# The opening of a two-layer decoder step: unit 0 and x in turns on one queue, squares on ScalarE, two more banks, five products of a cleared tile

## The reference

```python
def layer(i, h, ...):
    mix, buf_new, S_new = mixer(rmsnorm(h, norm1[i]), buf, S, pos0, w_in[i], ...)   # w_in: 1024 x 2560
    h = h + mix
    hn = rmsnorm(h, norm2[i])
    f = swiglu(hn, ...) if i % 2 == 0 else moe(hn, ...)    # 8 experts, top 2
    h = h + f
    gate = sigmoid(h @ w_ple_gate[i]); e = p_l @ w_ple[i]
    h = h + gate * e

def rmsnorm(x, g):
    y = xf * lax.rsqrt(jnp.mean(xf * xf, axis=-1, keepdims=True) + NORM_EPS)
    return y * g
```

## Time and profile before

| | us |
|---|---|
| median of 3 runs | 898.3 (895.4 to 898.36) |
| profiled execution | 897.86 |
| its span | 894.9 |
| TensorE busy in the span | 871.5 (97%) |
| VectorE, ScalarE, GpSimd busy | 692.8, 540.8, 172.9 |

### The profile page before, as it was taken

The page is one execution under the profiler, slowest core; times in us unless marked ns, Lnnn a source line. Parts: engine busy times, 40 slices in busy tenths (PEclk is TensorE's granted clock), DMA queues, the critical chain, the costliest instruction groups (busy, mean ns, idle before and its releaser), DMA issues.

```text
span 894.9 us, 14463 instructions
## 1 busy us (share of the span) xinstructions
PE 871.5 (97%) x5919; PEld 758.6 (85%) x5919; DVE 692.8 (77%) x793; ACT 540.8 (60%) x659; POOL 172.9 (19%) x190
## 2 busy tenths in 40 slices
PE   6999999999999999999999999999999999999995
PEld 5999999999999999999887777777777777777794
DVE  5796676555555588786869888899898989898976
ACT  5446555343435455346557878787777777876752
POOL 5456321100110013664411010002000110010012
PEclk9999999999999999998999999999999999999998
DMA  9993565545553644944439999999999999999801
GB/s 338 371 326 94 176 218 203 192 153 199 190 179 131 219 163 175 301 139 151 163 107 355 412 337 362 407 363 397 359 390 364 393 389 366 402 358 392 335 2 48
DMA packets 50739, 237.59 MB, mean 265 GB/s; under 512 B 4866, under 2 KB 8226, under 8 KB 42944
## 3 DMA queue, kind: packets, MB, share of 16 engines
q1 hardware_dynamic: 44672, 215.51, 64.5%
q0 software_dynamic: 5280, 20.04, 7.8%
q10 hardware_dynamic: 720, 1.10, 0.4%
HBM read 226.38 MB, written 9.63 MB: 264 GB/s over the span
## 4 chain that ended last, share of the span: by engine, by line
PE 79%; DVE 9%; DMA 4%; ACT 4%; issue 2%; POOL 1%; SPq 0%; ACTq 0%; DVEq 0%; POOLq 0%
PE bank L726 12%; PE bank L727 12%; PE bank L728 12%; PE bank L1091 8%; PE bank L1092 8%; PE bank L1093 8%; PE bank L1117 4%; PE bank L1116 4%; PE bank L1118 4%; DVE wlo L1575 4%; ACT whi L1282 2%; DMA raw<-in_moe_w_up 1%; DMA xg<-tokens,from_row 1%; PE bank L852 1%; PE bank L1049 1%
## 5 line engine op out<-in xcount | busy, mean ns | idle before, releaser
L1575 DVE TENSOR_TENSOR wlo<-raw,whi 128x1408 fp32r<-128x1408 f32 (+2 forms) x292 | 468.7, 1639 | 95.7 <-ACT whi L1282 95.6
L1282 ACT ACTIVATE whi<-raw 128x1408 fp32r<-128x1408 f32 (+2 forms) x292 | 392.5, 1377 | 146.0 <-PE bank L728 83.3
L726 PE MATMUL bank<-xh,whi 128*128 128x264 f32 x672 | 194.1, 289 | 9.3 <-DVE xl L1586 8.6
L727 PE MATMUL bank<-xl,whi 128*128 128x264 f32 x672 | 191.7, 285 | 0.0
L728 PE MATMUL bank<-xh,wlo 128*128 128x264 f32 x672 | 191.4, 285 | 0.0
L1091 PE MATMUL bank<-whi,xeh 128*96 128x512 f32 (+1 forms) x384 | 143.7, 374 | 0.7 <-DVE hid L1880 0.6
L1092 PE MATMUL bank<-wlo,xeh 128*96 128x512 f32 (+1 forms) x384 | 143.5, 374 | 0.0
L1093 PE MATMUL bank<-whi,xel 128*96 128x512 f32 (+1 forms) x384 | 143.2, 373 | 0.0
L726 PEld LDWEIGHTS bank<-xh,whi 128*128 128x128 f32 x672 | 127.8, 190 | 11.0 <-DVE wlo L1967 8.5
L727 PEld LDWEIGHTS bank<-xl,whi 128*128 128x128 f32 x672 | 127.9, 190 | 0.2
L728 PEld LDWEIGHTS bank<-xh,wlo 128*128 128x128 f32 x672 | 127.2, 189 | 0.0
(11 more groups left out here) (264 smaller groups left out, 1198.6 us busy)
## 6 DMA issues: line engine op xcount, KB each, us to landing
raw<-in_moe_w_gate SPq DMA_DIRECT2D x32, 1408.0 KB, 8.9
raw<-in_moe_w_up SPq DMA_DIRECT2D x32, 1408.0 KB, 9.4
raw<-in_moe_w_down SPq DMA_DIRECT2D x40, 1024.0 KB, 8.2
raw<-in_w_in SPq DMA_DIRECT2D x17, 1024.0 KB, 6.4
raw<-in_ffn_w_down SPq DMA_DIRECT2D x16, 704.0 KB, 4.3
raw<-in_ffn_w_gate SPq DMA_DIRECT2D x10, 1024.0 KB, 4.9
raw<-in_ffn_w_up SPq DMA_DIRECT2D x10, 1024.0 KB, 4.9
raw<-in_w_o SPq DMA_DIRECT2D x8, 1024.0 KB, 10.6
```

The source lines that it names most:

```text
L726: pe.matmul(out, w_hi, x_hi, start=start, stop=False)
L727: pe.matmul(out, w_hi, x_lo, start=False, stop=False)
L1282: act.activation(unit_hi(u), unit_raw(u), ACT.Copy).then_inc(hi_ready, 1)
L1575: dve.tensor_tensor(unit_lo(u), unit_raw(u), unit_hi(u).bitcast(F32), ALU.subtract).then_inc(lo_ready, 1)
```

## The change

- Unit 0 is loaded in four quarters (two rows of chunks each), and after each quarter two chunks of x, all on SyncE's queue; the first constants are issued behind unit 1. ScalarE's queue issues only the gains. Each quarter has its own semaphore; ScalarE and VectorE work quarter, two chunks of x, quarter and so on.
- All eight squares are made on ScalarE: two ahead of unit 1's halves, six behind them. GpSimd only adds.
- Chunks 4 and 5 (unit 2) use banks 5 and 6 instead of 0 and 1 and don't wait for an evacuation; the wait begins with chunk 6.
- TensorE first issues five fp32 products of the cleared tile `sq` into bank 7.

```diff
+FIRST_PARTS = (4, 2)
+        def unit_part(x, u, part, at=LOW_AT):
+            n = COLS[u] // FIRST_PARTS[u]
+            return x[:, at[u] + part * n:at[u] + (part + 1) * n]
+        def main_bank(n):
+            return n + 1 if n in (4, 5) else n % 4
...
-            first_rows(0, top_in)
-            first_rows(1, raw_landed[0])
-            sp.dma_start(const[:, 0:FIRST_CONST], t["const"][:, 0:FIRST_CONST]).then_inc(first_in, 16)
+            for i in range(4):
+                first_rows(i, top_in[i] if i < 3 else raw_landed[0])
+                sp.dma_start(h[:, 2 * i:2 * i + 2, :], t["x"][:, 2 * i:2 * i + 2, :]).then_inc(x_in[i], 16)
             for u in range(1, 3):
                 load_rows(u, t["w_in_rows"][:, 256 * u:256 * (u + 1)])
+                if u == 1:
+                    sp.dma_start(const[:, 0:FIRST_CONST], t["const"][:, 0:FIRST_CONST]).then_inc(first_in, 16)
...
-                if at >= 4:
+                if at >= 6:
                     pe.wait_ge(acc_free, n - 3)
-                out = bank[at % 4][:, 0:T]
+                out = bank[main_bank(at)][:, 0:T]
...
+            pe.wait_ge(still, 1)
+            for _ in range(5):
+                pe.matmul(bank[7][:, 0:T], sq[:, 0, 0:P], sq[:, 0, :], start=True, stop=True)
...
             act.dma_start(gains[:, :, :], t["gains"]).then_inc(gains_in, 16)
-            for i in range(4):
-                act.dma_start(h[:, 2 * i:2 * i + 2, :], t["x"][:, 2 * i:2 * i + 2, :]).then_inc(x_in[i], 16)
             act.wait_ge(still, 1)
             act.activation(rstd[0:1, 0:1], sq[0:1, 0, 0:1], ACT.Sqrt)
-            hi_half(0, 0)
-            for m in range(DC):
-                h_final(act, 0, m)
-                part(0, m)
-                if m == 1:
-                    hi_half(0, 1)
-            for half in range(2):
-                hi_half(1, half)
-            for m in range(5, DC):
-                act.activation(first[:, m, :], h[:, m, :], ACT.Square).then_inc(first_sq, 1)
+            for i in range(4):
+                hi_part(0, i)
+                for m in (2 * i, 2 * i + 1):
+                    h_final(act, 0, m)
+                    part(0, m)
+            for m in range(2):
+                first_square(m)
+            for i in range(2):
+                hi_part(1, i)
+            for m in range(2, DC):
+                first_square(m)
...
-            lo_half(0, 0)
-            for m in range(DC):
-                finish(0, m)
-                if m == 1:
-                    lo_half(0, 1)
-            for half in range(2):
-                lo_half(1, half)
+            for i in range(4):
+                lo_part(0, i)
+                for m in (2 * i, 2 * i + 1):
+                    finish(0, m)
+            for i in range(2):
+                lo_part(1, i)
...
             pool.memset(sq[:, 0, :], 0.0).then_inc(still, 1)
-            for m in range(5):
-                pool.wait_ge(x_in[m // 2], 16)
-                pool.tensor_tensor(first[:, m, :], h[:, m, :], h[:, m, :], ALU.mult).then_inc(pool_step, 1)
-                steps += 1
-            pool.wait_ge(pool_step, steps)
             for m in range(0, DC, 2):
-                if m >= 4:
-                    pool.wait_ge(first_sq, m // 2 * 2 - 3)
+                pool.wait_ge(first_sq, m + 2)
                 pool.tensor_tensor(first[:, m, :], first[:, m, :], first[:, m + 1, :], ALU.add).then_inc(first_sums, 1)
```

More of the change, by code:

```diff
@@ L652, in dense, with first_rows @@
                     load(first + j, t[name][layer][:, n * c0:n * (c0 + w)], n * w)
-            def first_rows(half, landed):
+            def first_rows(part, landed):
                 _, _, n, _, w = W_IN[0]
-                n //= 2
-                dst = unit_half(raw, 0, half).rearrange("p (k w) -> p k w", k=n)
-                src = t["w_in_rows"][half * n * P:(half + 1) * n * P, 0:w]
+                n //= FIRST_PARTS[0]
+                dst = unit_part(raw, 0, part).rearrange("p (k w) -> p k w", k=n)
+                src = t["w_in_rows"][part * n * P:(part + 1) * n * P, 0:w]
                 sp.dma_start(dst, src.rearrange("(k p) w -> p k w", p=P)).then_inc(landed, 16)
@@ L763, in first_pair @@
                 L = unit_lo(u).rearrange("p (k w) -> p k w", k=DC)
-                for half in range(2):
-                    pe.wait_ge(lo_ready if half else first_lo, u + 1)
-                    for k in range(4 * half, 4 * half + 4):
+                parts = FIRST_PARTS[u]
+                rows = DC // parts
+                for part in range(parts):
+                    if part == parts - 1:
+                        pe.wait_ge(lo_ready, u + 1)
+                    else:
+                        pe.wait_ge(first_lo, u * (FIRST_PARTS[0] - 1) + part + 1)
+                    for k in range(rows * part, rows * (part + 1)):
                         if u == 0:
@@ L774, in first_pair @@
                                 mm.then_inc(unit_used if m else acc_full, 1)
-                    if u and half == 0:
+                    if u and part == 0:
                         side_step(0, "norm1")
@@ L1436, in experts, with hi_part, first_square @@
                     part(5, m)
[L1438 to L1442 removed]
+            def hi_part(u, part):
+                last = part == FIRST_PARTS[u] - 1
+                act.wait_ge(raw_landed[LANDING[u]] if u or last else top_in[part], 16)
+                act.activation(unit_part(whi, u, part, HIGH_AT), unit_part(raw, u, part),
+                               ACT.Copy).then_inc(hi_ready if last else first_hi, 1)
+            def first_square(m):
+                act.activation(first[:, m, :], h[:, m, :], ACT.Square).then_inc(first_sq, 1)
             act.dma_start(gains[:, :, :], t["gains"]).then_inc(gains_in, 16)
[L1445 to L1446 removed]
             act.wait_ge(still, 1)
             act.activation(rstd[0:1, 0:1], sq[0:1, 0, 0:1], ACT.Sqrt)
[L1449 to L1458 removed]
+            for i in range(4):
[9 more added lines that the diff above has]
+                first_square(m)
             for l in range(DEPTH):
@@ L1962, in over_expert, with lo_part @@
                     dve.tensor_tensor(h[:, m, :], h[:, m, :], osg[:, :], ALU.add).then_inc(o_done, 1)
-            def lo_half(u, half):
-                dve.wait_ge(hi_ready if half else first_hi, u + 1)
-                dve.tensor_tensor(unit_half(wlo, u, half), unit_half(raw, u, half), unit_half(whi, u, half, HIGH_AT).bitcast(F32),
-                                  ALU.subtract).then_inc(lo_ready if half else first_lo, 1)
-            lo_half(0, 0)
-            for m in range(DC):
-                finish(0, m)
-                if m == 1:
-                    lo_half(0, 1)
-            for half in range(2):
-                lo_half(1, half)
+            def lo_part(u, part):
+                last = part == FIRST_PARTS[u] - 1
+                if last:
+                    dve.wait_ge(hi_ready, u + 1)
+                else:
+                    dve.wait_ge(first_hi, u * (FIRST_PARTS[0] - 1) + part + 1)
+                dve.tensor_tensor(unit_part(wlo, u, part), unit_part(raw, u, part), unit_part(whi, u, part, HIGH_AT).bitcast(F32),
+                                  ALU.subtract).then_inc(lo_ready if last else first_lo, 1)
+            for i in range(4):
[4 more added lines that the diff above has]
+                lo_part(1, i)
             for l in range(DEPTH):
```

13 lines of the change are left out of this document (3 added, 10 removed).

## The result

The changed kernel takes **899.15 us** (median of 14 runs, 896.8 to 903.5); the kernel before takes 896.84 (median of 14; one of them, 1073.8 us, is left out of every mean here). The ratio is 1.0029, with a 95% interval of 1.0016 to 1.0042: slower, by 1.4 to 3.8 us, a small loss but clear of the noise. The forecast was 897.1 against the profiled 897.9, a small gain. The profiled execution of after took 901.1 us, its span 899.4.

The account below looks back on a forecast made before the run. TensorE, busy 871.5 of 894.9 us, was taken as the bound. Unit 2 starting earlier gave -2.2 us, a clock fall +1.4, so -0.8 against the profiled 897.9: forecast 897.1, range 893.6 to 899.8.

Parts of the forecast that it names:

- nothing else in this diff touches the rest: Whole kernel behind the opening: nearly every microsecond TensorE gains in its opening comes off the end, nothing else changes.
- so the gain is kept: Weights after the opening: later loads have slack, ScalarE waits for TensorE and not a landing, so the -2.2 us stays.
- rival (2): Opening: the low clock stretch doubles to 6.7 us, price 3.4, net +1.2, giving 899.1 us; chance 0.15.
- The first product, unit 0's pieces: Opening: first product at about 5.9 us instead of 8.56; low parts of x at 0.43 to 0.48 us each.
- Unit 0's end: Opening: pairs land every 1.45 us, rounds come every 1.6, unit 0 ends at 11.9 us if cleared products raise the clock.
- The landing of unit 1: Opening: unit 1 lands at about 12.4 us at 367 GB/s, so TensorE begins it at 14.75 instead of 16.7.
- wrong if over 13: Sign against the forecast: unit 1 landing under 11.5 or over 13 us.
- The clock, the opening: Pause of some 2.9 us before unit 1: the clock falls for one low stretch of 3.4 us, costing +1.4 us.
- Sums of squares and banks: Opening: the norm waits 0 for the sums of squares; fresh banks for unit 2 save 0.25 us.

Follow-up runs that it names:

- e1: The changed kernel with five more fp32 products of the cleared tile in TensorE's pause between units 0 and 1; mean 897.32 us, ratio 1.0003.
- e3: The changed kernel with x issued on ScalarE's queue again, unit 0 still in quarters; 899.0 us, ratio 1.0017.
- e5: The changed kernel with unit 1 loaded in two halves, each with its own semaphore; 899.9 us, ratio 1.0029.
- e6: The changed kernel as it is, run and profiled again; mean 899.39 us, ratio 1.0024.
- e7: The changed kernel with the tenth unit of w_in and all later loads held until the second swap of q and k landed; 899.2 us, ratio 1.0026.
- e11: The changed kernel with its five cleared products cut to 64 rows and 2 columns; 899.2 us, ratio 1.0030.
- e2: The changed kernel without the five cleared products at the start; mean 896.91 us, ratio 1.0002.
- e12: The changed kernel without the five cleared products and with unit 1 loaded in two halves; 898.5 us, ratio 1.0020.
- e14: The changed kernel without the five cleared products, run a second time; mean 895.62 us, ratio 0.9994.
- e17: The changed kernel without the five cleared products, with one product of constants in the wait ahead of the window sums; 896.6 us, ratio 1.0000.
- e16: The changed kernel without the five cleared products, unit 1 in halves, three products of constants ahead of the window sums; 897.6 us, ratio 1.0010.
- e15: The changed kernel with 22 more products of 64 x 2 columns in the pause between units 0 and 1; 898.9 us, ratio 1.0019.

## Why the prediction was wrong, point by point

The step that failed is the sentence "nothing else in this diff touches the rest", with its twin "so the gain is kept": the places behind the opening stood in the sum with nothing, and they took about 2 of the 3.3 us between forecast and measurement. The opening's gain was also 1.0 us too large. The measured 899.15 is all but rival (2)'s 899.1, but that is luck: the rival has the whole loss in a doubled low stretch at the opening, and after's own profile, at 901.1 us, has a single one there.

- **The first product, unit 0's pieces: right.** 5.62 (said 5.9); a quarter costs ScalarE 0.63 (0.62) and VectorE 0.69 (0.72); the low parts, without GpSimd's squares beside them, 0.49:
```profile
L1605 DVE SCALAR_TENSOR_TENSOR xl<-h,gains,xh 128x264 fp32r<-128x264 f32 x8 | 3.6, 490 | 0.1
```
- **Unit 0's end: 12.79, said 11.9.** The pairs didn't land every 1.45 us but in pulses; TensorE stood from 7.02 to 8.11. It made the pause shorter, so it did no harm.
- **The landing of unit 1: wrong, 13.1 for 12.4.** The step took the 367 GB/s of the earlier trace rows for the whole transfer, and after moved less in four of the microseconds from 4 to 10 (263, 332, 309, 329). Over ten profiles it is 12.9, so part of the 0.7 is this execution's. It was listed as "wrong if over 13". Unit 1 gained 1.2 us instead of 1.95. The engines were saturated in before; that didn't say they would be with other transfers.
- **The clock, the opening: right in kind, too small in size.** The fall came, behind the pause, in each profile of after. The price taken was +1.4, one short stretch; 3 profiles have 3.4, 6.8 and 3.4 us, so the doubled stretch of rival (2), given 0.15, came in one profile of three, and the runs' own clock says +1.8 on the average over the whole kernel. That zeros raise the clock the rows couldn't show, and the forecast left both answers; they do.
- **Sums of squares and banks: right.** The sums were there before the norm wanted them; the bank wait went, 0.26 us (said 0.25).
- **"Later weights have slack, so the gain is kept": half right.** The slack of ScalarE and of the loads is there; that of VectorE in the rotation stage is not. From unit 2's first product to the window sums after takes 39.4 us for before's 38.4, and e1, whose opening has no fall, 39.0, so 0.6 us go there. Of a lead of 3.3 us 2.1 to 2.5 are gone by then, and a fall of the clock follows; of leads of 1.4 to 2.2 no more than 0.5. Before's own trace had the sign of it: VectorE busy 9.92 of the 10 us from 50 to 60, on the path behind which TensorE waits.
- **"Nothing else in this diff touches the rest": the step that failed.** The five products were costed at nothing, since they run in TensorE's idle start. 20 instructions more moved the code's fetches, +0.7 us at 812, which is shown, and +0.8 at 631, which is likely and varies from profile to profile. By the rests: +0.6 to +1.2 in the seven kernels with after's opening and 20 or 40 such instructions (after, e1, e3, e5, e6, e7, e11), -0.6 to -1.4 in four without (e2, e12, e14, e17), 1.9 us between the means; the spacings at 631 and 812 differ by 0.9 and 0.8 between the same two groups. e16, without the cleared products, has +1.0 and the longest wait at 631.

The sum as it came out, against before: opening without the fall -1.2 (e1's unit 2 at 23.46 for 24.62), rotation stage +0.6, the two late waits +1.5, together +0.9; the rest measured is +0.7. Clock +1.8. In all 2.7, measured 2.5. The terms of the first part come from single profiles (without a fall, and with unit 1 in one transfer, unit 2 started 1.0 to 2.2 us sooner than before) and the rest is good to 0.4, so their agreement is no proof of each of them. Against the forecast's -0.8 the miss of 3.3 us is 1.0 at the opening (-1.2 for -2.2, 0.7 of it the landing), 0.4 the clock's, 0.6 the rotation stage's and 1.5 that of the late waits, 3.5 in all.

What of the Trainium skill (TensorE: Matmul & The Clock Gate, HAM oscillation) was cited held for this pause: products in a burst with a wait for DMA behind them had the clock fall in all three profiles. The DMA waits of the page's own case are some 3 to 5 us long, these were 2.5 to 3.0; and behind pauses of 1.8 us (e3, e11, e14) the clock didn't fall, so "again each time" was too wide for this kernel. The page gave the term its sign, and the trace the size.

No kernel tried here is faster than before by more than its interval. The nearest is the change without the five products, 896.3 us over 24 runs against 896.8: -0.5, with an error of 0.5. So the rest of this change is worth about nothing that these runs can tell, and the five products cost 3.2 us.

## What to carry to other kernels

A lead gained at the start is worth what the next engine on the path lets through: follow the path to the next place where TensorE waits for another engine, or nearly does, and read that engine's busy share there, before the lead is booked to the end. A warm-up of TensorE that makes a pause for data longer can buy a low clock behind that pause; fill the pause or leave the warm-up out. And an instruction added in idle time isn't free in a program of thousands on an engine whose code is fetched while it runs: when two kernels differ by a few tenths of a per cent, compare the execution's granted clock first, and the waits far from the edit second.

## What the runs showed of the hardware

- Products of a cleared tile raise the clock as others do: it was up at 5.5 us, with them starting at 1.12 (4.4 us, as before from 8.56 to 13.0). With tiny ones (64 rows, 2 columns) it was up only at 10.0, within the 9.4 to 11.8 us of the kernels with none.
- Low stretches ahead of the one at the kernel's end are 3.4 or 6.8 us long in all 19 profiles, and the same kernel shows now one and now the other at the same place: after has 77.2 and 408.3, both of 6.8, before 3.4 and 6.7 at them. The row of after for the first:
```profile
77.20:84.00 6.80, 6.80 (x62) 6.56 (x60) 4.03 (x11) 6.52 (x28) 2.56 (x2) 0.50 0.06 23
```
  The mean clock goes with 64% of the variance between executions of one kernel: 0.91 us for 0.001.
- With one fetch of 16 KB of TensorE's code inside it, a load on GpSimd's queue took 10.5 to 11.1 us, without it 9.8 to 10.0.
- The first issue of one and the same indirect gather on GpSimd took 3.47 or 3.48 us in 18 profiles and 4.61 in e15, which differs from after by 22 tiny products on TensorE; why is open.
